# A hybrid decoder step on one core: table store and tile 0 moved in the front, modulation halves 4 to 11 spread from the end of stage A to stage C

## What is computed

```
m = silu(c) @ w_mod + b_mod          # w_mod is 1024 x 6144: six vectors of 1024 per group of c
sh1, sc1, g1, sh2, sc2, g2 = m       # c has 1 prompt row and 8 sample rows
h = x * (1 + sc1) + sh1              # needs the first two vectors only
z = h @ w_in                         # 1024 x 2328: pool | u | v | q | k,v | gates
...                                  # pooling, gating, attention with three branches
out = mix @ w_out
x = layer_norm(ALPHA * x + (1 + g1) * out)
h2 = x * (1 + sc2) + sh2             # the other four vectors are needed from here on
... mixture of 16 experts, layer_norm with g2 ...
```

## Time and profile before

| what | value |
| --- | --- |
| median of 3 runs | 1246.61 us (1242.82 to 1249.85) |
| profiled execution, its own time | 1253.85 us |
| profiled execution, span from first to last instruction | 1252.1 us |
| granted TensorE clock, mean share of full speed | 0.946 |
| PE busy | 1119.1 us, 89% of the span |
| DVE, ACT, POOL busy | 731.7, 587.6, 135.2 us |

### The profile page before, as it was taken

The page is one execution under the profiler, slowest core; times in us unless marked ns, Lnnn a source line. Parts: engine busy times, 40 slices in busy tenths (PEclk is TensorE's granted clock), DMA queues, the critical chain, the costliest instruction groups (busy, mean ns, idle before and its releaser), DMA issues. The chain is left out here.

```text
span 1252.1 us, 20501 instructions
## 1 busy us (share of the span) xinstructions
PE 1119.1 (89%) x7389; PEld 904.6 (72%) x7390; DVE 731.7 (58%) x1433; ACT 587.6 (47%) x1022; POOL 135.2 (11%) x203
## 2 busy tenths in 40 slices
PE   5699989998799999999889936999999999999844
PEld 3598879987666777778568725878888888888611
DVE  1461263243554777777676768885484588565157
ACT  0461100113465776766533235774475477555145
POOL 0212402010100000000000001020000011000061
PEclk9799999999997999999999967999999999999967
DMA  9645755054484300000343357996696599693488
GB/s 325 200 140 222 288 206 154 1 62 111 127 332 165 61 1 2 1 2 2 109 143 122 118 211 281 374 385 252 232 377 223 222 383 392 263 372 114 175 302 151
DMA packets 92343, 238.07 MB, mean 190 GB/s; under 512 B 8662, under 2 KB 18069, under 8 KB 92239
## 3 DMA queue, kind: packets, MB, share of 16 engines
q1 hardware_dynamic: 76153, 189.92, 43.2%
q0 software_dynamic: 10288, 31.20, 8.0%
q10 hardware_dynamic: 5830, 15.99, 3.6%
HBM read 199.04 MB, written 44.33 MB: 194 GB/s over the span
## 5 line engine op out<-in xcount | busy, mean ns | idle before, releaser
L2562 PE MATMUL psum<-w_hi,x_parts 128*128 128x512 f32 x736 | 239.7, 397 | 9.0 <-DVE x_parts L2681 9.0
L2674 DVE TENSOR_TENSOR w_lo<-raw,w_hi 128x2048 fp32r<-128x2048 f32 x95 | 213.3, 2286 | 44.7 <-ACT w_hi L2615 43.7
L2615 ACT CAST w_hi<-raw 128x2048 fp32r<-128x2048 f32 x90 | 167.6, 1914 | 29.3 <-DMA raw<-in_moe_w_gate 15.2
L2562 PEld LDWEIGHTS psum<-w_hi,x_parts 128*128 128x128 f32 x736 | 139.8, 190 | 39.8 <-issue 10.7
L2562 PE MATMUL psum<-w_lo,x_parts 128*128 128x512 f32 x368 | 144.7, 393 | 0.0
L2562 PE MATMUL psum<-w_hi,a_parts 128*128 x368 | 120.4, 399 | 4.0 <-DVE a_parts L2687 4.0
L1758 DVE CUSTOM_DVE_ANT_0 low<-psum,high 128x512 f32<-128x512 f32 (+5 forms) x172 | 92.2, 578 | 42.1 <-PE psum L1446 28.0
L1476 PE MATMUL psum<-keep,low 128*128 128x128 f32 (+1 forms) x556 | 95.0, 292 | 11.9 <-ACT high L1705 6.1
L1644 ACT ACTIVATE low<-low,high 128x640 f32<-128x640 f32 (+9 forms) x140 | 98.9, 709 | 9.9 <-DVE high L1758 9.6
L1671 ACT COPY high<-psum 128x512 f32<-128x512 f32 (+3 forms) x128 | 63.7, 502 | 81.5 <-PE psum L1476 81.3
L713 PE MATMUL psum<-h_hi,l_parts 128*128 128x384 f32 (+1 forms) x384 | 93.8, 327 | 0.0
(11 more groups left out here) (384 smaller groups left out, 1734.6 us busy)
## 6 DMA issues: line engine op xcount, KB each, us to landing
raw<-in_moe_w_gate SPq DMA_DIRECT2D x16, 2048.0 KB, 11.5
raw<-in_moe_w_up SPq DMA_DIRECT2D x16, 2048.0 KB, 11.0
raw<-in_moe_w_down SPq DMA_DIRECT2D x16, 2048.0 KB, 10.8
top<-in_w_mod SPq DMA_DIRECT2D x8, 2048.0 KB, 8.0
y_d<-work ACTq DMA_DIRECT2D x24, 512.0 KB, 5.8
low<-in_w_mod SPq DMA_DIRECT2D x4, 2048.0 KB, 18.9
high<-in_x_prompt SPq DMA_DIRECT2D x16, 512.0 KB, 3.9
y_d<-high SPq DMA_DIRECT2D x1, 8192.0 KB, 23.8
```

What stands on the lines that cost most here:

```text
L2562: mm = pe.matmul(out, left[l][:, k * P:(k + 1) * P], w[:, bass.ds(at - o + k * step, 512)], start=n == 0, stop=n == len(steps) - 1)
L2615: act.copy(c.w_hi[:, at:at + PART // 2], c.raw[:, o:o + PART // 2]).then_inc(hi_done[p], 1)
L2674: dve.tensor_tensor(low, c.raw[:, o:o + PART // 2], c.w_hi[:, at:at + PART // 2].bitcast(F32), ALU.subtract).then_inc(c.lo_done[p], 1)
```

## The change

```diff
-MOD_AFTER = {NT + 2: 4, NT + 4: 5, NT + 6: 6, NT + 8: 7, 2 * NT + 2: 8, 2 * NT + 4: 9, 2 * NT + 6: 10, 2 * NT + 8: 11}
+MOD_AFTER = {NT - 1: 4, NT + 1: 5, NT + 3: 6, NT + 5: 7, NT + 7: 8, 2 * NT + 1: 9, 2 * NT + 5: 10, 2 * NT + 8: 11}
...
-            for n in range(3):
-                mod_load(c, sp, n)
+            mod_load(c, sp, 0)
+            mod_load(c, sp, 1)
             load_x(0)
+            mod_load(c, sp, 2)
             mod_load(c, sp, 3)
+            load_x(1)
             for h in range(2):
                 load_w(h, KV0, WIDTHS[0], c.w_raw[0], slice(4 * h, 4 * h + 4))
-            load_x(1)
             load_x(2)
             sp.wait_ge(w_lo, A_UNITS)
             load_w(2, KV0 + WIDTHS[0], WIDTHS[1], c.w_raw[1])
...
             sp.wait_ge(w_lo, FIRST_UNIT[2])
-            for n in range(4, 8):
+            for n in range(4, 10):
                 mod_load(c, sp, n)
             sp.wait_ge(z_ready, 2 * NT)
             sp.wait_ge(w_lo, GROUP_UNIT)
             load_w(4, 0, 512, c.pu_raw)
-            for n in range(8, 12):
+            for n in range(10, 12):
                 mod_load(c, sp, n)
...
             gate_weights()
-            keep_busy(c, pe, 7, 12)
+            modulation_turn(0)
+            sample_gate_weights()
+            keep_busy(c, pe, 3, 12)
             mod_products(c, pe, 2)
-            sample_gate_weights()
+            transposes(0)
             keep_busy(c, pe, 3, 16)
             mod_products(c, pe, 3)
-            for v in range(2):
-                modulation_turn(v)
-            transposes(0)
+            modulation_turn(1)
             transposes(1)
...
-            act.wait_ge(tab_done, 1)
-            act.dma_start(c.tab_d, tab[0:NH, :].unsqueeze(1).to_broadcast([NH, TROWS, TABW])).then_inc(c.tab_out, 16)
             for u in range(4):
                 part_high(u)
             act.wait_ge(modT_done, 2)
...
             h_part(1)
+            act.wait_ge(tab_done, 1)
+            act.dma_start(c.tab_d, tab[0:NH, :].unsqueeze(1).to_broadcast([NH, TROWS, TABW])).then_inc(c.tab_out, 16)
             for n in range(2 * NT):
...
-                if st == 1 and i == 5:
+                if st == 1 and i == 3:
                     mod_vector(c, dve, 2)
+                if st == 1 and i == 7:
+                    mod_vector(c, dve, 3)
             for i in range(NT):
...
-                if i == 1:
-                    mod_vector(c, dve, 3)
-                if i == 5:
+                if i == 3:
                     mod_vector(c, dve, 4)
```

## The result

The changed kernel takes 1255.07 us (median of 14 runs, 1251.41 to 1259.01), the kernel before 1247.84 in runs beside it (14 runs, 1242.82 to 1252.74). The ratio is 1.0059, with a 95% interval of 1.0045 to 1.0073: 7.4 us slower, by 5.6 to 9.1. The forecast was 1.7 us slower, and no difference that can be told.

The account below looks back on a forecast made before the run. PE was taken to set the pace from about 47 us on, waiting for DMA before that. Terms -8.9 + 7.7 + 0.9 + 4.7 + 1.4 + 0.4 - 4.5 = +1.7 us on 1246.61 gave 1248.3 us, range 1241 to 1255.

Parts of the forecast that it names:

- three events: Signs of error: tile 3 landing within 9 us, half 4 there when PE comes, half 3's products ending after 36 us.
- step on halves 4 to 11: Stages A to C, moved modulation halves: new waits at halves 4 and 5, a low clock, stage C's waits gone.
- The front's gain, -8.9: Front, before the first product: without the store the loads land sooner, so ACT begins tile 0 8.9 us earlier.
- third rival: Front: low clock makes PE's work bind and natural(0) start 4 us later than in the sum; +5.7, 1252.3; chance 0.15.
- The store at tile 3, +7.7: Front, tile 3's load: the moved store on eight shared engines delays it 7.7 us; bounds 0 and +10.5.
- The clock behind tile 3, +0.9: After PE's longer wait for tile 3: a lower granted clock loses 0.9 us more, between 0 and 1.8.
- Half 4, +4.7: Behind stage A's last key transpose: PE waits 4.7 us for half 4; 3.2 with the shortest landing.
- The low clock behind half 4, +1.4: After PE's wait for half 4: the clock falls and costs another 1.4 us (0 to 3).
- Half 5, +0.4: Stage B: half 5's load meets the window state's copy and costs 0.4 us (0 to 3).
- second rival: Stage B: the window state's copy holds half 5 for 12.4 us, PE waits 3.1; +7.4, 1254.0; chance 0.17.
- Stage C, -4.5: Stage C: the four waits for halves 8 to 11 go, gaining 4.5 us (0 to -4.5).
- small errors cancelling: Whole kernel: the main forecast, two stalls traded for four small ones, spanning 1244 to 1252; chance 0.55.

Follow-up runs that it names:

- e1: Changed kernel with only the table's store put back ahead of the split of stage A's weights; ratio 1.0030.
- e4: Changed kernel with the table's store issued later still, by ACT after tile 6 is scaled in stage A; ratio 0.9964.
- e9: Changed kernel with the table's store cut in two, rows 8 to 15 of each head stored after tile 6 is scaled; ratio 1.0014.
- e2: Changed kernel with modulation halves 4 to 11 put back where the kernel before has them, the front staying changed; ratio 1.0002.
- e5: Changed kernel with POOL's two DRAM-to-DRAM copies (window state and pool state) issued after stage B's stores instead of before them; ratio 1.0047.
- e3: Kernel before with only modulation halves 4 to 11 moved as in the change; ratio 1.0045.
- e6: Changed kernel with 48 idle transposes on PE ahead of half 4's products; ratio 1.0077.
- e10: Changed kernel with both POOL copies behind stage B's stores and 40 idle transposes ahead of half 4's products; ratio 1.0048.
- e7: Kernel before with the changed front, but the table's store after tile 6 is scaled; halves 4 to 11 where they were; 1239.56 us, ratio 0.9926.
- e8: Kernel before with changed front, store after tile 6, halves 4 to 11 re-placed to their landings, halves 8 and 9 requested before the groups' weights; 1238.89 us, ratio 0.9931.
- e11: Kernel before with changed front, late store, halves fitted to their landings, plus 24 idle transposes between tile 1's transposes and the first product; ratio 0.9929.

## Why the prediction was wrong

Most mechanisms were the ones forecast, and none of the three events came that the forecast named as proof against itself (a landing of tile 3 within 9 us, half 4 there in time, half 3's products late). What failed is the sum: +1.7 us forecast, +7.4 measured. Most of it failed in the step on halves 4 to 11, with +2.0 forecast and +6.4 found at the groups; the rest in the store's cost at tile 3. The time itself, 1255.07, is only just beyond the range (1241 to 1255), and 1.2 us of its distance from 1248.3 is the kernel before, 1247.84 here against 1246.61 from three runs.

Term by term, measured for forecast: front -9.0 for -8.9, tile 3 +10.0 for +7.7, clock behind it +0.2 for +0.9, half 4 +6.0 for +4.7, slower work behind it +2.3 for +1.4, half 5 +1.4 for +0.4, stage C's waits for halves -4.5 for -4.5, and DVE +1.2 for nothing: +7.6 for +1.7.

- **The front's gain, -8.9.** Right: ACT began tile 0 at 35.19 (35.3 forecast), natural(0) at 38.12 (about 38). The high clock held through half 3's products (1.93 us at 30.87), so the third rival did not come; the clock did fall behind them, in the wait ahead of `natural(0)`.
- **The store at tile 3, +7.7.** This is the first step that failed, and the largest single term. Tile 3 took 10.0 us longer, near the upper bound (+10.5, the store's whole duration) and not the share of the eight engines. The step took the store's work per engine from the stretch 22.5 to 33, 62 engine-us, which gave 7.7. Beside tile 3 the same 136 packets took 25.2% of 16 engines for 17.8 us, 72 engine-us, or 9.0 on each of eight. The front came out at +1.0 us, not at -1.2. That the store does it is shown by e1, e4 and e9. e9 also shows that it is not simple proportion (3.2 us for half the bytes).
- **The clock behind tile 3, +0.9.** Too much for this execution: from tile 3 to the last key transpose of stage A only 0.2 us were lost (1.18 against 1.00). In e2, behind much the same wait, it was 1.2.
- **Half 4, +4.7.** 5.97 us. The place and kind were right, the landing was 10.4 and not 9.1. I had taken one landing as if it were fixed; half 4 landed in 8.0 to 11.4 us in these kernels, and what sets it is open.
- **The low clock behind half 4, +1.4.** Mis-sized: half 4's products alone lost 1.7 (3.64 against 1.93). From 97.65 to the groups the kernel lost 6.4 us; the waits there make 5.97 + 1.39 - 4.49 = 2.9, DVE's new ones 1.2, and what is left, about 2.3, is the slower work. I had carried over the price of a wait half as long, though the bounds (0 to 3) held it.
- **Half 5, +0.4.** 1.39 us in the wait, and it lands in 11.4. POOL's two copies are the cause: with both out of the way (e5) the landing is 7.5 and the wait none. That it is the window state's, 2 MB against 56 KB, is argued from the sizes. It is the mechanism of the second rival, at less than half of its price (3.1). That this rival's total, +7.4, is the measured one is luck: it needs a second low clock behind half 5, where the clock was 1.00 from 118 to 122 us, and it has nothing for DVE or for the store's larger cost.
- **Stage C, -4.5.** Right for the halves: none of these waits is left. e2, which puts them back, has 4.48 us of them again.
- **DVE, which has no term in the sum.** PE waits for it 0.58, 0.31 and 0.33 us in stage C and at the groups. These waits stand in every kernel with the changed order of the halves (e1, e3, e4, e5, e6, e9, e10) and in none with another (before, e2, e7, e8, e11), so they come with that order; by which step of it was not tried.

By the sum's own terms: the front was off by 2.2 - 0.7 = 1.5 us (tile 3's stall and the clock behind it, with the small rest to 97.65), and the halves by 4.4 (6.4 against 4.7 + 1.4 + 0.4 - 4.5 = 2.0). 1.7 + 5.9 is 7.6, which is what stands at the groups. By the ratios the front is even closer to its forecast, +0.2 us (e2) for -0.3, and the halves carry the whole miss, 5.6 us (e3) to 7.1 (the change less e2) for 2.0. The chances were off in the same way: I gave 0.55 to small errors cancelling, while half 4's wait was given a lower bound only, half 5 stood near the low end of its bounds, and stage C's gain at the best end of its own.

The Trainium skill (DMA: Bandwidth & Descriptors, "Queues, rings and completion order") has each engine take turns between the queues by the packet. That q1 and q10 moved 0.37 and 0.35 MB side by side from 50 to 58 us agrees with it in kind; the order of single packets is not shown here.

## What to carry to other kernels

A transfer taken off one critical load costs the next load that shares its engines. The price there was near its whole duration here (10.0 of 10.5 us), and less in proportion for half of it. Look for the stretch in which nothing is waited for: 26 us further on the store turned a loss of 0.6% into a gain of 0.4% (e4), and with the halves back in their places into one of 0.7% (e7). Before a consumer is moved forward, compare it with when its load can land: half 4's request was tied to another event, so moving its use three products ahead only made a wait, with a low clock behind it. And a landing time read from one place of a trace holds only for the traffic of that place.

## What was not expected of the hardware

- The clock fell behind waits of 2.01 us in e2 (products of 3.04 us) and 1.75 us in e7 (3.27), where a wait of 1.81 in the kernel before had none behind it; and it did not fall behind waits of 2.52 us in e1 and 3.69 us in e9. Over this range the length of a wait does not tell.
- Half 5 took 10.4 to 14.3 us to land where it was asked for soon behind the issue of POOL's copy of the window state: 3.8 us behind it in e9 (14.3), 5.2 in e1 (13.1), 5.5 in e6 (14.3), 7.1 in e3 (11.8), 7.4 in the changed kernel (11.4), 8.4 in e4 (10.7), 9.0 in e8 and e11 (10.4). In all eight it lands 18.1 to 19.8 us behind the copy's issue, so asking sooner wins little. Asked for 13.5 us behind it, in the kernel before, it took 7.6; with the copy moved away 7.5 in e5 and 8.7 in e10.
- Half of the store cost tile 3 3.2 us and all of it 10.0.
